# Down-projections of two expert layers: one eighth of the output taken from gathered expert rows

## What is computed

```
def peer(x, ...):                                  # block 2; block 1 has the same form
    idx, gate = ...                                # [token, 128]: the chosen experts and their softmax gates
    ue = jnp.take(u_tab, idx, axis=0)              # u_tab, v_tab: [16384, 2048], f32
    ve = jnp.take(v_tab, idx, axis=0)
    act = gelu(einsum('td,ted->te', x, ue))        # up-projection
    return einsum('te,ted->td', gate * act, ve)    # down-projection
```

## Time and profile before

| | us |
|---|---|
| median of 3 (4117.69 to 4121.73) | 4118.97 |
| the profiled execution, its own time | 4115.61 |
| its span, first to last instruction | 4113.8 |

### The profile page before, as it was taken

How to read it: one execution, slowest core, us unless ns; L and a number is a source line. 1 busy time by engine, 2 the same in 40 slices (tenths; PEclk the granted TensorE clock), 3 DMA queues, 4 the chain that set the end, 5 groups by cost and what they waited for, 6 DMA issues and landing times.

```text
span 4113.8 us, 70609 instructions
## 1 busy us (share of the span) xinstructions
PE 4056.4 (99%) x21364; PEld 3475.7 (84%) x21364; DVE 3177.4 (77%) x5534; ACT 2215.8 (54%) x3915; POOL 584.4 (14%) x509
## 2 busy tenths in 40 slices
PE   8999999999999999999999999999999999999998
PEld 8978898888888888888889899988888888888887
DVE  6477677996999766888769978698699986666666
ACT  5446544455666555555554465455566665555554
POOL 4100010000222222122210002000022222222221
PEclk9999999999999999999999999999999999999999
DMA  6434555666666666677755545466666666666664
GB/s 224 168 119 147 200 179 187 219 215 205 200 199 198 220 217 217 230 260 247 239 211 175 175 155 184 162 212 214 211 201 197 201 210 222 217 219 238 212 219 158
DMA packets 290795, 831.32 MB, mean 202 GB/s; under 512 B 25968, under 2 KB 93296, under 8 KB 287344
## 3 DMA queue, kind: packets, MB, share of 16 engines
q1 hardware_dynamic: 285728, 812.75, 58.9%
q10 hardware_dynamic: 4944, 17.06, 1.1%
HBM read 779.37 MB, written 50.33 MB: 202 GB/s over the span
## 4 chain that ended last, share of the span: by engine, by line
PE 93%; DVE 4%; ACT 1%; DMA 1%; issue 1%; SPq 0%; DVEq 0%; POOL 0%; ACTq 0%; POOLq 0%
PE psum L484 11%; PE psum L486 11%; PE psum L485 11%; PE psum L428 11%; PE psum L430 11%; PE psum L429 11%; PE psum L1744 5%; PE psum L1746 5%; PE psum L1745 5%; PE psum L1936 2%; PE psum L1938 2%; PE psum L1937 2%; PE psum L419 1%; DVE sb_w_lo L2325 1%; PE psum L1842 1%
## 5 line engine op out<-in xcount | busy, mean ns | idle before, releaser
L2025 ACT CAST sb_w_hi<-sb_raw 128x512 fp32r<-128x512 f32 x2736 | 1695.1, 623 | 1609.9 <-PE psum L486 646.8
L2325 DVE TENSOR_TENSOR sb_w_lo<-sb_raw,sb_w_hi 128x512 fp32r<-128x512 f32 x2736 | 1872.7, 711 | 847.2 <-ACT sb_w_hi L2025 838.7
L428 PE MATMUL psum<-sb_w_hi,sb_act_hl 128*128 128x512 f32 x2048 | 800.4, 391 | 5.2 <-DVE sb_w_lo L2325 4.9
L484 PE MATMUL psum<-sb_w_hi,sb_act_hl 128*128 128x512 f32 x2048 | 798.1, 390 | 3.0 <-DVE sb_w_lo L2325 1.6
L430 PE MATMUL psum<-sb_w_lo,sb_act_hl 128*128 128x512 f32 x2048 | 799.4, 390 | 0.0
L429 PE MATMUL psum<-sb_w_hi,sb_act_hl 128*128 128x512 f32 x2048 | 798.6, 390 | 0.0
L485 PE MATMUL psum<-sb_w_lo,sb_act_hl 128*128 128x512 f32 x2048 | 797.7, 390 | 0.0
L486 PE MATMUL psum<-sb_w_hi,sb_act_hl 128*128 128x512 f32 x2048 | 797.6, 389 | 0.0
L2291 POOL TENSOR_TENSOR sb_work<-sb_scratch,sb_work 128x256 f32 x256 | 304.5, 1190 | 1103.9 <-DVE sb_scratch L766 1103.9
L428 PEld LDWEIGHTS psum<-sb_w_hi,sb_act_hl 128*128 128x128 f32 x2048 | 384.7, 188 | 86.5 <-DVE sb_w_lo L2325 6.1
L1744 PE MATMUL psum<-sb_act_hl,sb_w_hi 128*128 128x256 f32 x1488 | 430.2, 289 | 26.4 <-DVE sb_w_lo L2325 13.8
(11 more groups left out here) (373 smaller groups left out, 4147.9 us busy)
## 6 DMA issues: line engine op xcount, KB each, us to landing
sb_raw<-in_u SPq DMA_DIRECT2D x512, 512.0 KB, 4.2
sb_raw<-in_v SPq DMA_DIRECT2D x512, 512.0 KB, 3.9
sb_raw<-in_w_z SPq DMA_DIRECT2D x82, 512.0 KB, 4.2
sb_raw<-in_w_gates SPq DMA_DIRECT2D x64, 512.0 KB, 3.5
acts_mid<-sb_up_acts SPq DMA_DIRECT2D x124, 256.0 KB, 5.5
sb_raw<-in_w_proj SPq DMA_DIRECT2D x56, 512.0 KB, 4.0
sb_raw<-in_w_q SPq DMA_DIRECT2D x48, 512.0 KB, 4.1
sb_raw<-in_w_branch SPq DMA_DIRECT2D x32, 512.0 KB, 4.0
```

Of the source, the lines that this page charges most:

```text
L428: pe.matmul(ps, h, w_hi[:, c, :], start=k == 0, stop=False)
L484: pe.matmul(ps, c_h, w_hi[:, c, :], start=first, stop=False, skip_group_check=True)
L2025: act.copy(w_hi[:, c, :], raw[:, 2 * par + c // 2, (c % 2) * 512:(c % 2) * 512 + 512]).then_inc(hi_ready, 1)
L2325: dve.tensor_tensor(w_lo[:, c, :], raw[:, 2 * par + c // 2, (c % 2) * 512:(c % 2) * 512 + 512], w_hi[:, c, :].bitcast(F32), ALU.subtract). ...
```

## The change

The last 512 columns (`c = 3`) of the first 128 tokens (`t = 0`) no longer come from the dense product; `out_tile` leaves these three matmuls out, and has 21. For each of the 128 tokens POOL gathers instead the 128 chosen rows of the table, cut to their last 512 columns (a new input `picked_v1`, `picked_v2`), with one indirect DMA: 128 rows of 2 KB, one on each partition. A second indirect DMA fetches from `acts_mid` for each of the 128 experts the run of 32 acts (128 B) in which the token's act lies. All other columns, all other tokens, the loads of `v` and the splits stay as they were.

Tokens go in groups of four (`quad`, 32 per block: tokens q, 32 + q, 64 + q, 96 + q). DVE picks the act out of its run, multiplies it with the gate, and places it in column `q` of a [128 x 32] block of zeros (`place`, five instructions). PE multiplies each of the four blocks with its gathered rows, in plain f32, into 32 partitions of psum bank 6 (`quad`, four matmuls). DVE makes the two index tables in the first three tiles of the stage (`make_indices`).

Two tables set the order. `PICKS` lists the 256 indirect DMAs of a block; 15 of them follow each 7 `weigh`s of POOL, from tile 3 on. `quad_tile` puts `place(q)` on DVE and `quad(q)` on PE two tiles behind the tile of the quad's last DMA. There are buffers for three quads (`QUAD_SLOTS`), in rows 2 to 15 of `act_hl`, which the down stage does not use. The loops of PE, DVE and POOL in these stages are written out; ACT's and SP's are not. Some semaphores of other stages are merged to make room (`table_stored` and `table_loaded` with `x_loaded`, `masks_loaded` with `glu_loaded`).

```diff
+def pick_tile(k):
+    return 3 + k * 7 // 15
+def quad_tile(q):
+    return pick_tile(8 * q + 11) + 2
+PICKS = [("rows", 0, j) for j in range(4)]
+for quad_before in range(QUADS):
+    PICKS += [("rows", quad_before + 1, j) for j in range(4)] if quad_before + 1 < QUADS else []
+    PICKS += [("acts", quad_before, j) for j in range(4)]
...
-                    for t in range(QT):
+                    for t in range(QT) if c < 3 else (1,):
...
-            out_tile(0, 0, True)
-            tiles(pe, 1, 128, lambda i, u: out_tile(i, (1 + u) % 2, False))
+            def quad(q):
+                n = q % QUAD_SLOTS
+                pe.wait_ge(lone_ready, QUADS * (blk - 1) + q + 1)
+                for j in range(4):
+                    mm = pe.matmul(psum[32 * j:32 * j + 32, 6, :], lone[:, n, j, :], picked[:, 4 * n + j, :],
+                                   start=q == 0, stop=False, skip_group_check=True)
+                mm.then_inc(quad_used, 1)
+            for i in range(128):
+                out_tile(i, i % 2, i == 0)
+                for q in QUADS_AFTER[i]:
+                    quad(q)
...
+            def place(q):
+                n = q % QUAD_SLOTS
+                wide = [P, 4, RUN]
+                lane = iota[:, 0:RUN].unsqueeze(1).broadcast_to(wide)
+                dve.wait_ge(picked_loaded[n], 128 * len(range(n, QUADS, QUAD_SLOTS)) * (blk - 1) + 128 * (q // QUAD_SLOTS + 1))
+                link(dve.tensor_tensor(coef_parts, lane, by_quad(lanes)[:, q, :].unsqueeze(2).broadcast_to(wide), ALU.is_equal))
+                link(dve.tensor_tensor(coef_parts, picked_runs[:, n], coef_parts, ALU.mult))
+                link(dve.tensor_reduce(picked_coef[:, 0, :], coef_parts, AX.X, ALU.add))
+                link(dve.tensor_tensor(picked_coef[:, 1, :], picked_coef[:, 0, :], by_quad(slots[:, 0, 0:P])[:, q, :], ALU.mult))
+                if q >= QUAD_SLOTS:
+                    dve.wait_ge(quad_used, QUADS * (blk - 1) + q - QUAD_SLOTS + 1)
+                dve.tensor_tensor(lone[:, n], picked_coef[:, 1, :].unsqueeze(2).broadcast_to(wide),
+                                  one_of[:, 31 - q:63 - q].unsqueeze(1).broadcast_to(wide), ALU.mult).then_inc(lone_ready, 1)
+            def step(i):
+                lows(i, i % 8, i < 126)
+                next(indices, None)
+                for q in QUADS_AFTER[i]:
+                    place(q)
...
-                tiles(pool, 0, 128, weigh)
+                def pick(kind, q, j):
+                    n, at = q % QUAD_SLOTS, 32 * j + q
+                    if kind == "rows":
...
+                        if q >= QUAD_SLOTS and j == 0:
+                            pool.wait_ge(quad_used, QUADS * blk + q - QUAD_SLOTS + 1)
+                        pool.indirect_dma_start(picked[:, 4 * n + j, :], None, v_rows,
+                                                bass.IndirectOffsetOnAxis(ap=v_index[:, at:at + 1], axis=0)).then_inc(picked_loaded[n], 16)
+                    else:
...
+                        if q >= QUAD_SLOTS and j == 0:
+                            pool.wait_ge(lone_ready, QUADS * blk + q - QUAD_SLOTS + 1)
+                        pool.indirect_dma_start(picked_runs[:, n, j, :], None, runs,
+                                                bass.IndirectOffsetOnAxis(ap=run_index[:, at:at + 1], axis=0)).then_inc(picked_loaded[n], 16)
+                for i in range(128):
+                    weigh(i, i % 2)
+                    for kind, q, j in PICKS_AFTER[i]:
+                        pick(kind, q, j)
```

More of the change, by code:

```diff
@@ L27 @@
 UP_GROUPS = 32
+PICKED = 512
+QUADS, QUAD_SLOTS, RUN = 32, 3, 32
 REPLACED = -3e38
@@ L56, in tile_bases @@
     return base, evac
+def pick_tile(k):
[6 more added lines that the diff above has]
+    PICKS += [("acts", quad_before, j) for j in range(4)]
+PICKS_AFTER = [[pick for k, pick in enumerate(PICKS) if pick_tile(k) == i] for i in range(128)]
+QUADS_AFTER = [[q for q in range(QUADS) if quad_tile(q) == i] for i in range(128)]
 def rope_and_masks():
@@ L251, in build_two_blocks @@
         peer_keys2 = flat(48, 49).rearrange("p (q n) -> p q n", q=2)
-        x_loaded = [sem(f"x_loaded{c}") for c in range(4)]
+        x_loaded = [sem(f"x_then_tables{c}") for c in range(4)]
+        table_stored, table_loaded = x_loaded[0:2], x_loaded[2:4]
+        picked_loaded = [sem(f"picked_loaded{n}") for n in range(QUAD_SLOTS)]
         consts_loaded, small_loaded, cols_loaded = sem("consts_loaded"), sem("small_loaded"), sem("cols_loaded")
@@ L315, in build_two_blocks @@
         table_in, table_ready = sem("table_in"), sem("table_ready")
-        table_stored = [sem(f"table_stored{j}") for j in range(2)]
-        table_loaded = [sem(f"table_loaded{j}") for j in range(2)]
         xs_done, xs_used, s_ready = sem("xs_done"), sem("xs_used"), sem("s_ready")
@@ L777, in dve_experts @@
             turn_tile(1, 1)
+            indices = make_indices()
             first = 0
             if blk == 1:
-                eights(dve, 0, 40, lows)
+                for i in range(40):
+                    step(i)
                 first = 40
                 for _ in dve_s5_tables(dve, link):
-                    lows(first, first % 8)
+                    step(first)
                     first += 1
-                eights(dve, first, 106, lows)
+                for i in range(first, 106):
+                    step(i)
                 first = 106
                 for _ in dve_s5_inputs(dve, link):
-                    lows(first, first % 8)
+                    step(first)
                     first += 1
-            eights(dve, first, 126, lows)
-            lows(126, 6, False)
-            lows(127, 7, False)
+            for i in range(first, 128):
+                step(i)
             if blk == 1:
```

65 lines of the change are left out of this document (55 added, 10 removed).

## The result

The changed kernel takes **4053.07 us** (median of 4 runs, 4049.81 to 4056.15) against 4118.33 (4 runs of the kernel before beside it): a ratio of 0.984, with an interval of 0.9823 to 0.9857. The forecast was 4026 us, 2.3% less; the gain is 1.6%. The profiled execution takes 4052.76 us, its span is 4050.9.

What follows compares the result with a forecast made beforehand. PE was taken as the bound, busy 99% of the span. 4115.6 - 174.0 (matmuls) + 76.8 (quads) + 4 (DVE) = 4022.4 us, a median of 4026 us with the 3.4 us offset; 8-in-10 range 3998 to 4110.

Steps and rivals of the forecast that it cites:

- PE loses 174 us, gains 77 us: PE in both down stages: 768 matmuls go, saving 174.0 us; 64 quads at 1.2 us come in, costing 76.8 us.
- DVE's `place`: DVE in the down stages: five instructions, 1.29 us a quad, 0.35 us per tile; 4.85 us a tile in v1's tiles 40 to 105.
- The quad's own wait is covered: Down stages: `place` ends 2.6 us into PE's tile and PE reaches the quad at 4.76, so no wait.
- I charge 4 us there; ends 0 and 10: Tiles 40 to 105 of v1: DVE stays under PE with little room for table bursts; 4 us charged, between 0 and 10.
- DMA engines: Gathers add 35.7 MB a block, 106 us of all 16 engines by bytes, 278 by packets; bytes taken, 537 of 650 us, hidden.
- A stage uses 0.62 x 696 = 431 us: DMA engines' use in a down stage before the change: a share of 0.62, 431 us of 696.
- DMA rival: DMA engines fill up in the down stages, loads come late: 4145 us by packets, some 4050 to 4110 halfway; chance 0.10.
- POOL: POOL in the down stages: a gather takes 1.2 us, POOL is busy 3.8 of 5.08 us a tile, gathers cost nothing.
- the rival at 4343 us: Down stages: POOL becomes the bound if a gather exceeds 1.80 us; at 2.43 us the kernel takes 4343 us; chance 0.15.
- The quads one at a time: PE in the down stages: a quad's matmuls don't run side by side, 198 instead of 77 us, kernel 4147 us; chance 0.03.
- the likeliest case: Whole kernel: PE still the bound, 4026 us, own range 3994 to 4062; chance 0.72.
- the sign that was set for "wrong": Down stages: PE idle in front of L515, put down to `w_lo` or `act_hl`, would show the forecast wrong; no size given.

Runs made afterwards that it cites:

- nogather: The changed kernel with only each block's first three quads fetching rows and acts, 24 gathers a block instead of 256: 4027.7 us (1 run).
- spread: The changed kernel with block 1's gathers at 1.4 a tile in tiles 40 to 105, three elsewhere, quads one tile behind their last gather: 4042.0 us.

## Why the prediction was right, and where it failed

- **PE loses 174 us, gains 77 us: right.** v2 shows it without anything else: 650.1 against 647.2 us. A quad costs 1.20 us (forecast 1.2). Of the 2.9 us too many, 1.5 are the first matmuls of the stage, 0.43 us apart, and 0.6 a pause at 3746.2. These matmuls follow a wait of 2.44 us (0.69 before) for ACT's last acts of the stage in front:

```profile
3375.79 0.80 PE L515 MATMUL psum<-sb_w_hi,sb_act_hl 128*128 128x512 f32 x1 [2.44 <-ACT sb_last_acts L580]
3376.39 0.63 PE L516 MATMUL psum<-sb_w_lo,sb_act_hl 128*128 128x512 f32 x1
3376.81 0.63 PE L517 MATMUL psum<-sb_w_hi,sb_act_hl 128*128 128x512 f32 x1
```

- **DVE's `place`: right in size.** The five instructions take 0.281 + 0.292 + 0.286 + 0.166 + 0.292 = 1.32 us (1.29). In tiles 40 to 105 DVE needs 4.86 us of a tile (309.5 us from 1660 to 2000, 63.75 tiles), and 4.85 was forecast. But PE's tile there is 340 / 63.75 = 5.33 us, not 5.08: PE waits though no engine is full. nogather has 4.78 of 5.13. "The quad's own wait is covered" failed in v1: there the 32 quads cost 42.4 us on PE and not 38.4, and with `place` cut to one instruction (light) these 4.0 us are gone. In v2 it held.
- **"I charge 4 us there; ends 0 and 10": the step that failed.** It weighed means against means and charged the bursts only. v1 came out 25.3 us over its 653.4. What the runs show in its place: 6.0 us for `lam`, 4.9 for the small instructions, 8.8 for row bytes, 10.1 for gathers that crowd the table stretch; 29.8 if they were separate, but they overlap (21.0 became 16.0, since spread shortens the pause of `lam` too). Both single items are in the kernel before already. PE lost 1.0 and 1.1 us in the first two windows of the earlier trace rows; 0.5 of the first lies ahead of the stage's first matmul, and the rest are, on the timeline of before, a pause at the same load of `lam` and one at the same small instructions:

```profile
1624.10 0.50 PE L484 MATMUL psum<-sb_w_hi,sb_act_hl 128*128 128x512 f32 x1 [0.44 <-DVE sb_w_lo L2325]
...
1663.65 0.51 PE L484 MATMUL psum<-sb_w_hi,sb_act_hl 128*128 128x512 f32 x1 [1.15 <-DVE sb_w_lo L2325]
```

They should have been priced. My reading, argued and not shown: with PE's tile 0.4 us shorter and DVE's 0.3 longer, ACT and DVE no longer build up the lead of most of a tile that hid such waits.
- **DMA engines: the count right, the stage wrong.** By bytes the addition was to be 106 us a block; the page's q0 has 5.5% of the span, 111 us a block. (Its packets are 28,672, where the prediction counted 65,536.) "A stage uses 0.62 x 696 = 431 us" is v2's share. The row above it in the earlier trace rows has 0.71 and 247 GB/s for the table stretch of v1. By the same count, 247 x 5.44 / 5.08 + 59 (35.7 MB in 119.5 tiles of 5.08 us) makes 323 GB/s, a share of 0.93. Measured: 0.88 and 308, at a longer tile. Loads "land later than 3.9 us": 4.9. In v2, at 0.86, ACT waits 13 us for them, and PE loses hardly anything by it (0.4 us of waits for `w_lo`): DVE has 487.6 / 118.5 = 4.11 us of work in a tile of 5.06. In v1, with 4.86, PE pays. So the DMA rival's "loads begin to come late" was true, and cost time in one stage.
- **POOL: right.** In v2 it is busy for 388 of 600 us, where near three quarters were forecast. A gather takes 1.09 to 1.18 us in the mean (1.2 forecast), 2.0 at most, and POOL waits for quads 268 us, while PE never waits for POOL and ACT only at the start of each stage (1.1 and 2.0 us): the rival at 4343 us did not come. The weighing became shorter, 965 ns instead of 1219, and DVE's instructions beside it longer.
- **The quads one at a time** did not come: eight records in 1.06 us.

The range (3998 to 4110) held the time; the likeliest case's own range (3994 to 4062) did too, by its allowances (late loads up to 20 us, DVE up to 10), not by its sum. Its condition, PE without gaps, held in v2 alone. In v1 the sign that was set for "wrong" showed: PE in front of L515 waits 19.7 us for `w_lo`, and behind that ACT waits 41.4 us for `in_v`.
